# Context FFN in a two-block transformer kernel: high and low activation parts side by side in one 512-column product

## The reference

```python
def swiglu(h, w13, w2):
    a, b = jnp.split(h @ w13, 2, axis=-1)
    return (jax.nn.silu(a) * b) @ w2

def half_ffn(x, g, shift, scale, gate, w13, w2):
    return x + 0.5 * gate * swiglu(modulate(x, g, shift, scale), w13, w2)

cs = half_ffn(cs, norm_g[i, 0], mc[:, :, 0], mc[:, :, 1], mc[:, :, 2], ffn_w13[i, 0], ffn_w2[i, 0])
```

## Time and profile before

| | |
|---|---|
| median of three executions | 3318.3 us |
| profiled execution, its own time (span) | 3318.5 us |
| PE matmul busy | 3268.5 us, 98% |
| DVE, ACT, POOL busy | 1904.3, 1274.1, 806.2 us |
| stage `ctx_ffn`, first matmul to the end of slab 33 | 1319.7 to 1513.5 us |
| granted clock of TensorE in that stage | 1.00 |

### The profile page before, as it was taken

The page is one execution under the profiler, slowest core; times in us unless marked ns, Lnnn a source line. Parts: engine busy times, 40 slices in busy tenths (PEclk is TensorE's granted clock), DMA queues, the critical chain, the costliest instruction groups (busy, mean ns, idle before and its releaser), DMA issues.

```text
span 3318.5 us, 49003 instructions
## 1 busy us (share of the span) xinstructions
PE 3268.5 (98%) x17840; PEld 2800.1 (84%) x17840; DVE 1904.3 (57%) x2520; ACT 1274.1 (38%) x1924; POOL 806.2 (24%) x501
## 2 busy tenths in 40 slices
PE   7989999999999999999999999999999999999999
PEld 6769888888888888998888977888898888998887
DVE  5467766654477766567656666665553355363233
ACT  4464433354553334544322446322242223442221
POOL 1111222111112222533323132232223231113321
PEclk9999999999999999999999999999999999999999
DMA  4112433321224333545544311453432243222222
GB/s 148 70 38 102 148 137 127 115 104 51 89 93 161 129 132 115 182 178 186 201 146 167 135 52 39 147 197 145 158 112 92 101 162 111 102 89 89 101 93 97
DMA packets 69904, 401.71 MB, mean 121 GB/s; under 512 B 7520, under 2 KB 10224, under 8 KB 31216
## 3 DMA queue, kind: packets, MB, share of 16 engines
q1 hardware_dynamic: 46400, 317.80, 26.8%
q10 hardware_dynamic: 23344, 81.73, 7.0%
HBM read 397.41 MB, written 2.10 MB: 120 GB/s over the span
## 4 chain that ended last, share of the span: by engine, by line
PE 96%; DVE 2%; issue 1%; ACT 1%; DMA 0%; SPq 0%; DVEq 0%; ACTq 0%
PE banks L540 25%; PE banks L541 25%; PE banks L542 25%; PE banks L446 3%; PE banks L447 3%; PE banks L448 3%; PE banks L557 2%; PE banks L559 2%; PE banks L558 2%; PE banks L673 1%; PE banks L891 1%; PE banks L928 1%; PE banks L916 1%; PE banks L804 1%; PE banks L644 0%
## 5 line engine op out<-in xcount | busy, mean ns | idle before, releaser
L540 PE MATMUL banks<-h_hi,whi 128*128 128x512 f32 (+1 forms) x2752 | 1039.0, 378 | 1.4 <-DVE h_lo L2309 0.9
L542 PE MATMUL banks<-h_hi,wlo 128*128 128x512 f32 (+1 forms) x2752 | 1033.6, 376 | 0.0
L541 PE MATMUL banks<-h_lo,whi 128*128 128x512 f32 (+1 forms) x2752 | 1033.6, 376 | 0.0
L2339 POOL TENSOR_TENSOR wlo<-raw,whi 128x512 fp32r<-128x512 f32 (+1 forms) x281 | 442.0, 1573 | 2183.1 <-ACT whi L1002 2183.1
L540 PEld LDWEIGHTS banks<-h_hi,whi 128*128 128x128 f32 x2752 | 518.1, 188 | 100.7 <-issue 6.3
L541 PEld LDWEIGHTS banks<-h_lo,whi 128*128 128x128 f32 x2752 | 518.2, 188 | 94.0 <-issue 1.7
L542 PEld LDWEIGHTS banks<-h_hi,wlo 128*128 128x128 f32 x2752 | 518.1, 188 | 93.7
L1002 ACT ACTIVATE whi<-raw 128x1024 fp32r<-128x1024 f32 x281 | 296.3, 1055 | 522.2 <-PE banks L542 518.8
L1578 DVE TENSOR_TENSOR wlo<-raw,whi 128x1024 fp32r<-128x1024 f32 x281 | 469.0, 1669 | 38.8 <-ACT whi L1004 38.8
L540 PE MATMUL banks<-mid_hi,whi 128*128 128x512 f32 (+1 forms) x1136 | 423.6, 373 | 2.3 <-issue 2.3
L541 PE MATMUL banks<-mid_lo,whi 128*128 128x512 f32 (+1 forms) x1136 | 423.2, 373 | 0.0
(11 more groups left out here) (295 smaller groups left out, 4216.4 us busy)
## 6 DMA issues: line engine op xcount, KB each, us to landing
raw<-stream SPq DMA_DIRECT2D x298, 1024.0 KB, 4.8
mraw<-mod_stream ACTq DMA_DIRECT2D x144, 512.0 KB, 3.4
x<-xT SPq DMA_DIRECT2D x8, 256.0 KB, 5.7
out<-x SPq DMA_DIRECT2D x8, 256.0 KB, 2.1
ka<-k_a ACTq DMA_DIRECT2D x1, 1600.0 KB, 8.3
ko<-k_odd ACTq DMA_DIRECT2D x1, 1152.0 KB, 5.2
crow<-c_rows ACTq DMA_DIRECT2D x1, 1024.0 KB, 6.8
cx<-ctxT SPq DMA_DIRECT2D x1, 1024.0 KB, 7.6
```

What stands on the lines that cost most here:

```text
L540: mm(o, hi, a_hi[:, kc, 0:T], start=(kc == 0), stop=False)
L541: mm(o, hi, a_lo[:, kc, 0:T], start=False, stop=False)
L542: last = mm(o, lo, a_hi[:, kc, 0:T], start=False, stop=(kc == K - 1))
L2339: G.tensor_tensor(wlo[:, slot, 0:wd], raw[:, slot, 0:wd], whi[:, slot, 0:wd].bitcast(F32), ALU.subtract)\
```

## The change

The context's normalised activations go to a new place, `h_ctx` = slot 1 of `mid_lo`: for each kc, 256 columns of high parts and behind them 256 columns of low parts. The middle activations of the context lie so too: the low parts go to the upper 256 columns of `mid_hi`. For the context, `slab_out` then makes two products in place of three: high weights by all 512 columns, and low weights by the 256 high columns, into columns 0 to 255 of the bank. The sum that is wanted is the bank's left half plus its right half. After each slab ACT copies the right halves of both banks to `cg` (`copy_low`, 128 x 2 x 256), and DVE adds the left halves to that (`add_low`, 128 x 2 x 256). Silu, the product with the value half and the addition to `cx` then read `cg`.

```diff
+        h_ctx = mid_lo[:, 1]
...
+                        if T == CTX:
+                            both = acc[slot][j][:]
+                            if kc == 0:
+                                mm(both, hi, a_hi[:, kc, :], start=True, stop=False)
+                                mm(o, lo, a_hi[:, kc, 0:T], start=False, stop=False)
+                            else:
+                                mm(o, lo, a_hi[:, kc, 0:T], start=False, stop=False)
+                                last = mm(both, hi, a_hi[:, kc, :], start=False, stop=(kc == K - 1))
+                            continue
                         mm(o, hi, a_hi[:, kc, 0:T], start=(kc == 0), stop=False)
                         mm(o, hi, a_lo[:, kc, 0:T], start=False, stop=False)
                         last = mm(o, lo, a_hi[:, kc, 0:T], start=False, stop=(kc == K - 1))
...
+            def copy_low(s, i2=0):
+
+                act.wait_ge(slab_done, s + 1 + i2)
+                A(cg[:, s % 2, :].rearrange("p (j n) -> p j n", j=2), pairs[s % 2][:, :, CTX:], ACT.Copy)\
+                    .then_inc(ctx_low, 1)
...
                         act.wait_ge(stg_ready, n - 1 + i2)
+                        if T == CTX:
+                            copy_low(s, i2)
+                            act.wait_ge(ctx_sum, s - s0 + 1 + i2)
+                            g = cg[:, s % 2, 0:T]
                         A(sg[:, b, 0:T], g, ACT.Silu).then_inc(silu_done, 1)
                     split_next(s, i2)
...
                 for i in range(4):
+                    if T == CTX:
+                        copy_low(s0 + 16 + i)
                     split_next(s0 + 16 + i)
...
+            def add_low(s, i2=0):
+
+                dve.wait_ge(slab_done, s + 1 + i2)
+                dve.wait_ge(ctx_low, s - slab_of("ctx_ffn") + 1 + i2)
+                both = cg[:, s % 2, :].rearrange("p (j n) -> p j n", j=2)
+                V.tensor_tensor(both, pairs[s % 2][:, :, 0:CTX], both, ALU.add).then_inc(ctx_sum, 1)
...
                 dve.wait_ge(slab_done, s[0] + i + 1)
+                if T == CTX:
+                    add_low(s[0] + i)
+                    dve.wait_ge(ctx_sum, s[0] + i - slab_of("ctx_ffn") + 1)
...
+                    if T == CTX:
+                        ps = cg[:, (s[0] + i) % 2, j * T:j * T + T]
...
+                    elif T == CTX:
+                        add_low(s, i2)
+                        right = cg[:, s % 2, T:]
                     else:
                         right = v[:, 0:T]
...
-                            G.tensor_tensor(mid_lo[:, slot_mid, bass.ds(2 * i + j, 1), 0:T],
+                            dst = mid_lo[:, slot_mid, bass.ds(2 * i + j, 1), 0:T]
+                            if T == CTX:
+                                dst = mid_hi[:, slot_mid, bass.ds(2 * i + j, 1), T:]
+                            G.tensor_tensor(dst,
```

More of the change, by code:

```diff
@@ L305, in build @@
         ctx_loaded = sem("ctx_loaded")
+        ctx_low = sem("ctx_low")
+        ctx_sum = sem("ctx_sum")
         mod_loaded = [sem("mod_loaded0"), sem("mod_loaded1")]
@@ L583, in ffn @@
                 s, n0 = slab_of(name), SPLIT[name][0]
+                a_hi, a_lo = (h_ctx, None) if T == CTX else (h_hi, h_lo)
                 if not lead:
-                    slabs(s, 2, h_hi, h_lo, DC, T, split0=split_h)
+                    slabs(s, 2, a_hi, a_lo, DC, T, split0=split_h)
                 if middle:
                     stat(middle, 0)
-                slabs(s + 2, 6, h_hi, h_lo, DC, T)
-                slabs(s + 8, 8, h_hi, h_lo, DC, T)
+                slabs(s + 2, 6, a_hi, a_lo, DC, T)
+                slabs(s + 8, 8, a_hi, a_lo, DC, T)
                 slabs(s + 16, 4, mid_hi[:, 0], mid_lo[:, 0], 8, T, split0=n0)
-                slabs(s + 20, 6, h_hi, h_lo, DC, T)
+                slabs(s + 20, 6, a_hi, a_lo, DC, T)
                 slabs(s + 26, 4, mid_hi[:, 1], mid_lo[:, 1], 8, T, split0=n0 + 8)
@@ L1052, in unit_hi @@
                 dst, y = half_cols(norm, h_hi[:, c, :], a), class_blocks(norm, stgh[:, u % 4, :])
+                if norm == "ctx0":
+                    dst = h_ctx[:, c, 0:CTX]
                 if shift is None:
@@ L1205, in ffn @@
                 for i in range(4):
+                    if T == CTX:
+                        copy_low(s0 + 26 + i)
                     split_next(s0 + 26 + i)
@@ L1213, in last_round @@
                 for i in range(4):
+                    if s0 == slab_of("ctx_ffn", 30):
+                        copy_low(s0 + i)
                     split_next(s0 + i)
@@ L1624, in unit_lo @@
                 dst, shift = half_cols(norm, h_lo[:, c, :], a), norm_shift(norm, c)
+                if norm == "ctx0":
+                    hi, dst = h_ctx[:, c, 0:CTX].bitcast(F32), h_ctx[:, c, CTX:]
                 if shift is None:
```

## The result

The changed kernel takes 3335.35 us (median of five, 3335.09 to 3339.57) against 3318.3: the ratio is 1.0051, 95% interval 1.0041 to 1.0062. The forecast was 3331.6 with a range of 3325 to 3337.

A forecast was written before the change was run, and what follows sets the result against it. PE was taken to bound the kernel, with hardly any reserve in the context FFN's two-slot ring. -7.2 + 0.7 + 8.2 + 5.6 + 6.0 = +13.3 us gave 3331.6 us, range 3325 to 3337.

The forecast's parts named there:

- The ring and its margins: Context FFN's two-slot ring: PE wants slab s + 2 at D + 5.50; margins 1.5 us, 0.2 with a table load.
- What PE gains: Context FFN, 528 pairs of products: each 0.3464 us in place of 0.360, together -7.2 us.
- Up slabs: Split ready at D + 5.40, wanted at D + 5.28: 0.12 us wait at six up slabs, +0.7 us.
- Table loads: First loop: Copy and Silu each load a table per pass, split 2.70 us late three times, +8.2 us.
- rival A: First loop: the Copy draws no table load of its own, each wait shrinks by 1.28, 3327.8 us; chance 0.26.
- First down round: DVE needs 6.93 us per slab against PE's 5.54, so PE waits at slabs 19 to 22: +5.6 us.
- Second and last round: Same DVE period against last-round slabs of 4.16 us: 8.6 us of waits, +6.0 us net.
- The clock: PE's clock in the context FFN read as 1.00 from the earlier trace; the sum has no term for it.
- Rivals C and D: C: down rounds don't queue, only up slabs pay, 3320 us, chance 0.08. D: ring holds everywhere, 3311.1 us, 0.04.
- Rival B: Copy and addition cost 0.9 us each on DVE's side beside POOL's work: +4 more, 3336 us; chance 0.10.

The follow-up runs named there:

- its control: The kernel before the change plus a single one-column Silu behind the inverse root of m00: 3319.22 us (1.0001).
- the two without the sum: Changed kernel without copy and addition: 3316.41 us with the products alternating, 3316.71 us with both 512-column products first per kc.
- the last one: Changed kernel with two products only in up slabs 0-15 and 22-25, Silu's table preloaded, part of the split moved ahead of Silu and product: 3317.07 us (0.9995).
- the four with longer gaps: The changed kernel (3335.35 us), and it with Silu's table preloaded (3330.67), down slabs undone (3324.91), or the x-normalising units left out (3322.26).

## Why the prediction was right, step by step

- **The ring and its margins: shown.** With copy and addition gone the gaps fall from 22.2 us to 5.3 (stage 190.65); with the units gone the gaps after slabs 18 to 21, 28 and 29 go (0.2 us stays after slab 21); with the loads gone two of their three gaps go.
- **What PE gains: mis-sized.** Predicted -7.2, measured -4.6 in the changed kernel and -5.3 without the sum. A pair takes 0.3495 us and not 0.3464. The 0.7 between the two go, as far as I can see, in good part where PE restarts behind a gap: the second matmul of such a slab starts 0.30 us after the first (1371.31 and 1371.61 in slab 8), in place of 0.23. The 6 cycles of the Trainium skill (TensorE: Matmul & The Clock Gate, Back-to-back issue gap), which gave 1.3 us, are further off.
- **Up slabs: +0.7 predicted, +1.4 measured.** The split is ready at D + 5.47 (1377.31 to 1382.78) and PE starts at D + 5.56 (1382.87), where I had 5.40 for it: the copy's reader starts 0.70 after the copy and not 0.63, the last part ends 4.05 after Silu's start and not 4.00, and PE follows 0.09 later and not 0.05.
- **Table loads: +8.2 predicted, +6.5 measured.** Two loads per pass, as expected, so rival A fell, and with it, for a body entered with the table unknown, the step from "copy is in every set", as the Trainium skill has it (ScalarE: Activation LUTs, Table sets: the hidden batching unit), to "Copy needs no load". The term that was off is the second load, which I had put behind the wait for the sum.
- **First down round: +5.6 predicted, +5.8 measured**, single gaps 0.76, 1.38, 1.38, 2.11 predicted against 0.96, 1.41, 1.41, 2.03. DVE's period is 7.12 and not 6.93: the residual takes 0.50 us more than in the earlier trace rows and the first part of `wlo` 0.40 less, and the wait for the copy is 0.18 in place of 0.10.
- **Second and last round: +6.0 predicted, +5.0 measured.** Of the second gap of 2.76 only 1.3 came: slab 31 itself ran 1.6 us longer at half clock, which covered the rest. So the clock's net price there is about nothing, and its loss in slab 6 is the real one.
- **The clock: 0 predicted, +3.2 measured.** I took 1.00 from the earlier trace rows and did not ask what gaps of 2 to 3 us do to it. The kernels in whose stage no gap reaches 2 us show no half clock in it (before, its control, the two without the sum, the last one); the four with longer gaps do, once or twice. But of the 13 gaps of 2.0 to 2.9 us in those four only five were followed by one, and elsewhere shorter ones were: in the changed kernel half clock begins at 202.7 us, behind 1.31 us of idle time, there among small matmuls. That the gaps bring it is read from these nine traces and was not tried by itself, and which gap does I can't say.
- **Sum.** -4.6 + 19.1 + 3.2 = 17.7 in the stage against +13.3. The waits were right in kind and 1.4 us too high (20.5 against 19.1); PE's gain was 2.6 too high, and the clock was missing. Rivals C and D needed margins that the trace before denied, and fell. Rival B (0.9 for each new step) fell too: the addition took 0.69 and the copy 0.60. Even with POOL at work all through it (1370.09 to 1371.80) an addition took 0.68 (1371.13), as the argument that these are PSUM reads had it.
- **Where luck came in.** The measured 3335.35 lies 3.8 over the forecast and inside the range, but the range reached to 3337 only for rival B, which did not come about. The 3.2 us of half clock that filled that room stood in no rival.

## What to carry to other kernels

A stage in which PE is busy 99% of the time can have no reserve at all behind it: in a two-slot ring, work out when the next-but-one slot is wanted and when it is ready, for each kind of slot. A change that takes 0.2 us of PE per slab and puts 1.35 us in series between a slab's end and the next split must be checked against that margin, and against the occupancy of the engine that serves the slot. Where new work must be added as the banks are read out, put what releases the next slot ahead of its readers in the queues: here the split came at D + 4.56 in place of 5.47.

## What the runs showed of the hardware that I had not expected

- In the middle of an otherwise full stage, PE ran at 1.2 GHz for 3.4 us behind five of thirteen gaps of 2.0 to 2.9 us, beginning within 1.2 us of PE's return. Each time it cost some 1.6 us of matmul time (slab 6: 7.02 against 5.40).
- In this stage a 512-column float32r matmul takes 0.233 us by starts, and one of 256 columns 0.115 to 0.117. Among equal neighbours 512 columns take 0.2268 in the next stage, and 256 took 0.120 in this stage before the change.
- An operation on DVE with both operands in SBUF pays for POOL's work beside it: the product into `stg` took 0.43 us alone and 0.97 beside POOL (1377.92 in the last experiment), where the addition with one operand in PSUM took 0.68 beside it and 0.69 alone. The residual pair took 1.37 with POOL beside it for 0.92 us and 1.10 with POOL for 0.43 (1520.33); the 0.87 from PSUM in the earlier trace rows had POOL beside it for 0.28 only, so these do not compare the two sources.
